# Two-block network on one core: gated attention's level differences one level ahead, one Ln and Exp for two tiles, feed-forward norm tile by tile

## What is computed

```python
def hybrid_layer(x, ...):
    h = rms_norm(x, norm_mix)
    proj = h @ w_in                      # queries, keys, values, gates of four mixers
    y_nsa, y_sb, y_gla, y_fox = ...      # four attention mixers
    branch = jnp.einsum('bsnc,ncd->bsnd', ys, w_branch)
    gates = jax.nn.sigmoid(gate_logits + b_gate)
    x = x + jnp.sum(gates * branch, axis=2) @ w_out
    h2 = rms_norm(x, norm_ff)
    return x + jnp.square(jax.nn.relu(h2 @ w_ff1)) @ w_ff2
```

## Time and profile before

| what | us |
|---|---|
| median of 3 runs | 2266.33 |
| the profiled execution's own time | 2267.46 |
| its span in the profile | 2265.7 |
| VectorE busy | 1250.2 (55%) |
| ScalarE busy | 675.4 (30%) |
| GpSimd busy | 480.4 (21%) |

### The profile page before, as it was taken

The page is one execution under the profiler, slowest core; times in us unless marked ns, Lnnn a source line. Parts: engine busy times, 40 slices in busy tenths (PEclk is TensorE's granted clock), DMA queues, the critical chain, the costliest instruction groups (busy, mean ns, idle before and its releaser), DMA issues.

```text
span 2265.7 us, 32730 instructions
## 1 busy us (share of the span) xinstructions
PE 2185.9 (96%) x13766; PEld 1777.7 (78%) x13766; DVE 1250.2 (55%) x1678; ACT 675.4 (30%) x1496; POOL 480.4 (21%) x259
## 2 busy tenths in 40 slices
PE   7999999999999999999999999999999999998998
PEld 7998878889889987788898745557888886556987
DVE  5576445855455765448654316664434434456666
ACT  2224453032012234450330267622112012362111
POOL 2222112323322221123233000101111110101332
PEclk9999999999999999999999999999999999999999
DMA  9533666645465336676546403022232223213551
GB/s 264 182 121 119 254 248 194 246 149 223 168 171 207 136 126 222 229 238 218 191 183 218 172 0 118 1 74 93 75 111 84 102 65 85 86 62 120 196 186 56
DMA packets 225958, 339.57 MB, mean 150 GB/s; under 512 B 58987, under 2 KB 94806, under 8 KB 225814
## 3 DMA queue, kind: packets, MB, share of 16 engines
q1 hardware_dynamic: 224720, 333.98, 42.7%
q0 software_dynamic: 944, 3.47, 0.4%
q10 hardware_dynamic: 150, 0.04, 0.0%
HBM read 335.38 MB, written 2.10 MB: 149 GB/s over the span
## 4 chain that ended last, share of the span: by engine, by line
PE 58%; DVE 3%; ACT 2%; issue 1%; POOL 0%; DVEq 0%; ACTq 0%; POOLq 0%
PE bank L2118 15%; PE bank L282 13%; PE bank L284 13%; PE bank L283 13%; PE bank L2121 2%; PE bank L655 2%; DVE ring_low L270 1%; PE bank L1000 1%; ACT work L1134 1%; PE bank L658 1%; PE bank L952 0%; ACT work L2419 0%; DVE work L1693 0%; ACT work L2517 0%; ACT L1134 0%
## 5 line engine op out<-in xcount | busy, mean ns | idle before, releaser
L283 PE MATMUL bank<-hT_high,ring_low 128*128 128x256 f32 (+1 forms) x2048 | 608.3, 297 | 0.0
L283 PEld LDWEIGHTS bank<-hT_high,ring_low 128*128 128x128 f32 x2048 | 393.4, 192 | 12.1 <-issue 0.7
L263 POOL CAST ring_high<-ring 128x2048 fp32r<-128x2048 f32 (+1 forms) x108 | 204.1, 1890 | 685.8 <-PE bank L284 620.7
L282 PE MATMUL bank<-hT_low,ring_high 128*128 128x256 f32 (+1 forms) x1008 | 296.6, 294 | 7.5 <-DVE ring_low L270 4.5
L270 DVE TENSOR_TENSOR ring_low<-ring,ring_high 128x2048 fp32r<-128x2048 f32 (+1 forms) x108 | 242.1, 2244 | 98.4 <-POOL ring_high L263 98.2
L284 PE MATMUL bank<-hT_high,ring_high 128*128 128x256 f32 (+1 forms) x1008 | 286.4, 284 | 0.0
L263 POOL CAST half_high<-ring 128x2048 fp32r<-128x2048 f32 x64 | 128.4, 2009 | 638.2 <-PE bank L284 465.4
L282 PE MATMUL bank<-ring_low,hidden_high 128*128 128x512 f32 x640 | 251.4, 393 | 0.0
L1134 ACT ACTIVATE work<-bank 128x384 f32<-128x384 f32 (+11 forms) x246 | 109.4, 466 | 364.5 <-PE bank L284 314.8
L282 PEld LDWEIGHTS bank<-hT_low,ring_high 128*128 128x128 f32 (+1 forms) x1008 | 193.5, 192 | 16.7 <-issue 9.2
L270 DVE TENSOR_TENSOR ring_low<-ring,half_high 128x2048 fp32r<-128x2048 f32 x64 | 152.7, 2390 | 97.0 <-POOL half_high L263 96.6
(11 more groups left out here) (242 smaller groups left out, 4424.3 us busy)
## 6 DMA issues: line engine op xcount, KB each, us to landing
ring<-w_ff SPq DMA_DIRECT2D x32, 2048.0 KB, 8.2
ring<-mlp_w SPq DMA_DIRECT2D x32, 2048.0 KB, 8.0
ring<-w_in SPq DMA_DIRECT2D x30, 2048.0 KB, 8.6
ring<-w_ada SPq DMA_DIRECT2D x20, 2048.0 KB, 8.9
ring<-w_branch SPq DMA_DIRECT2D x24, 512.0 KB, 6.4
ring<-w_in SPq DMA_DIRECT2D x32, 256.0 KB, 4.2
ring<-w_out SPq DMA_DIRECT2D x4, 2048.0 KB, 8.8
work<-w_ada SPq DMA_DIRECT2D x4, 2048.0 KB, 13.5
```

The costliest lines, as they stand in the source:

```text
L263: nc.gpsimd.tensor_copy(self.high(i), self.part(i, False)).then_inc(self.high_made, 1)
L282: nc.tensor.matmul(out, a[0], b[1], start=start, stop=False)
L283: nc.tensor.matmul(out, a[1], b[0], start=False, stop=False)
```

## The change

1. `prepare(n)` is cut into `decay(n)`, the difference, and `scale_qk(n)`, the scalings. The difference of the next level is issued right behind the scalings of a level, ahead of the low half and the merge.
2. ScalarE takes Ln and Exp of the gated output's statistics once for both tiles, after the squares of tile 1; VectorE's scaling of both tiles waits for that one event.
3. Norm of the feed-forward: `take_hT` and `low_bits` go tile by tile; ScalarE copies the modulation sums after them; TensorE's `turn_ada` (and the rows) come behind the first product of up0.
4. VectorE makes only low half 0 ahead of `add_out(1, 0)`, half 1 behind the low parts; GpSimd's casts of halves 2 and 3 wait for the scaled tile 1 instead of `wo11`.
5. Second block: the semaphore `kpe_zero` is replaced by a count on `kpe_ready`.

```diff
@@ tensor
         turn_x("yT", 1, TT + 2, xn)
-        turn_ada()
-        if l == DEPTH - 1:
-            pe.wait_ge(rows3_in, 2 * 16)
-            turn(OT.claim(pe, "rows3")[:, 0:N_ROWS3], rows3[0:N_ROWS3, :]).then_inc(OT.full, 1)
         arrived = columns("yT", 6)
...
                 last.then_inc(PROJ.full, 1)
+                if i + b == 0:
+                    turn_ada()
+                    if l == DEPTH - 1:
+                        pe.wait_ge(rows3_in, 2 * 16)
+                        turn(OT.claim(pe, "rows3")[:, 0:N_ROWS3], rows3[0:N_ROWS3, :]).then_inc(OT.full, 1)
@@ scalar
-            link(f(gl_stat[:, t], gl_stat[:, t], ACT.Ln, scale=1.0 / GLA_DV, bias=eps))
-            f(gl_rstd[:, t], gl_stat[:, t], ACT.Exp, scale=-0.5).then_inc(gl_scale, 1)
+        link(f(gl_stat, gl_stat, ACT.Ln, scale=1.0 / GLA_DV, bias=eps))
+        f(gl_rstd, gl_stat, ACT.Exp, scale=-0.5).then_inc(gl_scale, 1)
...
         row_scale(lambda t: PROJ.taken(act, f"wo0{t}", f"wo1{t}"), sq)
+        for t in range(TT):
+            for c in range(2):
+                take_hT("yT", ROW_FF, hT_high[1], c, t)
         ps = OT.arrived(act, "ada")
         copy(ada_sums, ps[:, :]).then_inc(OT.free("ada"), 1)
-        for c in range(2):
-            for t in range(TT):
-                take_hT("yT", ROW_FF, hT_high[1], c, t)
@@ gpsimd
-        pool.wait_ge(*done("wo11"))
+        pool.wait_ge(xn_ready, TT + 2)
@@ vector
-        prepared = [0]
-
-        def prepare(n):
-            h, k = LEVELS[n], prepared[0]
-            prepared[0] += 1
+        prepared = [n for n in range(len(LEVELS)) if LEVELS[n] > 0]
+
+        def decay(n):
+
+            h, k = LEVELS[n], prepared.index(n)
...
                               b[:, :, h - 1:h].to_broadcast([P, 512 // (2 * h), 2 * h]), ALU.subtract).then_inc(lv_diff, 1)
+
+        def scale_qk(n):
+
+            k = prepared.index(n)
+            d = lv_d[:, k % 2]
             dve.wait_ge(lv_exp, k + 1)
...
-        prepare(0)
+        decay(0)
         Y.make_low(nc, dve, 15)
-        prepare(2)
-        for n in range(2):
-            Y.make_low(nc, dve, 16 + n)
-            merge(n)
+        scale_qk(0)
+        decay(2)
+        Y.make_low(nc, dve, 16)
+        scale_qk(2)
+        merge(0)
+        decay(3)
+        Y.make_low(nc, dve, 17)
+        merge(1)
         for n in range(3, len(LEVELS)):
-            prepare(n)
+            scale_qk(n)
+            if n + 1 < len(LEVELS):
+                decay(n + 1)
             Y.make_low(nc, dve, 15 + n)
             merge(n - 1)
...
-            dve.wait_ge(gl_scale, t + 1)
+            dve.wait_ge(gl_scale, 1)
...
-        X.make_low(nc, dve, 0, 1)
+        X.make_low(nc, dve, 0)
         add_out(1, 0)
         norm(0, TT + 1, xn)
         add_out(1, 1)
         norm(1, TT + 2, xn)
-        for c in range(2):
-            low_bits("yT", ROW_FF, hT_high[1], c)
-        X.make_low(nc, dve, 2, 3)
+        for t in range(TT):
+            for c in range(2):
+                low_bits("yT", ROW_FF, hT_high[1], c, t, TT * KD + (TT * t + c) * 4)
+        X.make_low(nc, dve, 1, 2, 3)
```

More of the change, by code:

```diff
@@ L1420, in sigmoid, with low_bits @@
             link(vec.reciprocal(e, e))
[L1422 to L1435, removed]
+        def low_bits(name, row, high, c, t, rounded_before):
+            ps = TURN[t].arrived(dve, f"{name}{t}{c}")
+            dve.wait_ge(hT_rounded, rounded_before + 4)
+            for k in range(4):
+                at, part = row + 4 * c + k, slice(t * P, (t + 1) * P)
+                last = vec.scalar_tensor_tensor(hT_low[:, 4 * c + k, part], ps[:, k * P:(k + 1) * P], cols[:, at:at + 1],
+                                                high[:, 4 * c + k, part].bitcast(F32), ALU.mult, ALU.subtract)
+                if k == 3:
+                    last.then_inc(TURN[t].free(f"{name}{t}{c}"), 1)
+                elif t == TT - 1:
+                    last.then_inc(hT_cut, 1)
         if l > 0:
@@ L1442, in vector @@
         for c in range(2):
-            low_bits("xT", ROW_MIX, hT_high[0], c)
+            for t in range(TT):
+                low_bits("xT", ROW_MIX, hT_high[0], c, t, (TT * c + t) * 4)
             if l == 0 or c == 1:
@@ L2066, in second_block @@
     kpe_ready = sem("kpe_ready")
-    kpe_zero = sem("kpe_zero")
+    KPE_ZEROED, KPE_ROTATED = 1, 2
     ln_order = [(i, j, t) for i in range(DEPTH) for j in range(2) for t in range(NT[i])]
@@ L2246, in mla_project @@
                     PT.taken(pe, "1sumk")
-                    pe.wait_ge(kpe_zero, 1)
+                    pe.wait_ge(kpe_ready, KPE_ZEROED)
                     pe.wait_ge(grid_in, 16)
@@ L2670, in mla_project @@
         def mla_project():
-            vec.memset(m_kpe[0:HD, :], 0.0).then_inc(kpe_zero, 1)
+            vec.memset(m_kpe[0:HD, :], 0.0).then_inc(kpe_ready, 1)
             for t in range(TT):
@@ L2687, in mla_project @@
                    lambda ps: ps[pe_rows, 0:S]).then_inc(kpe_ready, 1)
-            dve.wait_ge(kpe_ready, 1)
+            dve.wait_ge(kpe_ready, KPE_ROTATED)
             for j in range(1, 8, 2):
@@ L2875, in gpsimd @@
         norm_rows(1, 0, whole_count[0, 1, TT - 1])
-        pool.wait_ge(kpe_ready, 1)
+        pool.wait_ge(kpe_ready, KPE_ROTATED)
         for n in range(4):
```

## The result

The changed kernel takes 2248.05 us (median of 4 runs, 2246.20 to 2249.92) against 2265.65 us (4 runs): ratio 0.993, interval 0.9913 to 0.9947. Six more runs of it in a later experiment gave 2247.43 us and 0.9919 (0.9903 to 0.9935). So it is faster by some 18 us; forecast were 20.6 us and 2247 us.

The account below looks back on a forecast made before the run. TensorE bounds the kernel, busy for 2185.9 us, so only its idle time can be won. 3.4 + 1.4 + 7.3 + 8.5 = 20.6 us off 2267.46 gives 2246.9, said as 2247 us; range 2241 to 2259.

Parts of the forecast that it names:

- Levels: Gated-attention levels: the earlier difference shortens TensorE's waits for VectorE's merges, 1.7 us a layer, 3.4 us in all.
- some 0.5 us of the 1.13 stay: TensorE's wait before level 8: the merge of level 7 still comes late, leaving some 0.5 us of 1.13.
- my walk: VectorE's new queue in the levels followed through the old cast times, each low half behind its cast, to date the merges.
- Statistics: Gated output: two table loads, one Ln, one Exp fewer; TensorE's 0.42 and 0.30 us waits go, 1.4 us in all.
- Norm: Feed-forward norm: TensorE's idle before the first product falls to 1.1 us in each layer, 7.3 us together.
- the first low part at 459.4, and TensorE starts at 459.5: Layer 0, first feed-forward product: it starts right after tile 1's first low part, with 1.1 us idle.
- Clock: TensorE's half-clock stretches behind the waits in levels and norm: 10.2 us as upper bound, 8.5 us taken as gain.
- Rival (a): The idle goes and the clock still falls: 2255.4 us at worst, 2251 where half stays; chance 0.2.
- (b): Feed-forward norm: GpSimd's casts, released with tile 1's scaled rows, hold the low parts of hT; 2260 us, chance 0.05.
- (d): Slower: differences and scalings meet a cast at each level, some 13 us more a layer, 2276 us; chance 0.03.

Follow-up runs that it names:

- levels_only: Kernel before with the difference of a level issued one level ahead, nothing else: 2258.39 us against 2264.47, ratio 0.9977 (0.9966 to 0.9988).
- own_banks: Changed kernel with tile 1 turned into the two SC banks instead of PROJ's: median 2246.08 us of five, ratio 0.9914 to the kernel before.
- stats_only: Kernel before with one Ln and one Exp for both tiles of the gated output, nothing else: 2261.70 us, ratio 0.9991 (0.9980 to 1.0001).

## Why the prediction was right, and where its terms were not

The direction, the size and the range were right: 2247 forecast, 2248.05 and 2247.43 measured. That the time was met so closely is in part luck: the sum hides errors that cancel in part, and its 20.6 us, 3 too many, were taken off one execution that lay 1.8 us above the median of four (2267.46 against 2265.65).

- **Levels: 3.4 us forecast; 4.6 us of waits for merges and 1.84 us of waits for ScalarE's bank gone.** The step "some 0.5 us of the 1.13 stay" failed: the changed kernel and levels_only have no wait at level 8. In levels_only the merge of level 7 starts 4.1 us behind the end of its cast; my walk had 5.2, since it put the whole piece of the compressed branch, 1.7 us, behind the cast, while 0.6 us of it ran ahead and only 0.7 us were left behind it. And the walk looked at VectorE's and TensorE's own waits only; the label "issue" hid ScalarE's bank.
- **Statistics: 1.4 us**, as forecast, by the profile. The reading behind it was off in one place: three of the four instructions had a table load ahead, not all four; two loads a layer are gone all the same.
- **Norm: 7.3 us of idle forecast, 5.4 gone** (4.73 and 4.78 us to 2.07 each). The step "the first low part at 459.4, and TensorE starts at 459.5" failed. The product claims the PROJ bank that holds tile 1's turned rows, and so waits for the fourth low part; own_banks gave 0.72 of the missing 0.97 us back. The steps before it held: the additions, the 0.75 us scaling, both turns without waits. From the end of the output products to the first feed-forward product it is 7.9 us, where 7.1 were forecast.
- **Clock: 8.5 us forecast, about 2.6 measured, give or take 1.2.** This is the term that was most off. Even if all the 10.2 us of lost clock in those stretches had gone, at 0.61 they would have brought 6.2. The profiled execution of before had falls behind level 8 in both layers and behind both norms. I took them as the waits' price in every run. In stats_only, which keeps the waits at levels 7 and 8 (1.01 and 1.19 us, level 8 at 182.56), the stretch in question is

```profile
182.00:188.00 6.00, 5.44 (x48) 5.35 (x49) 4.59 (x5) 0.01 (x1) 1.53 (x1) 1.00 0.01 3
```

  at full clock, and so is the one behind level 8:

```profile
184.00:190.00 6.00, 6.00 (x51) 5.88 (x50) 3.22 (x3) 0.00 (x0) 0.00 (x0) 1.00 0.00 0
```

  And of the changed kernel's two profiles one has no fall behind the norms (the stretch 452 to 462 has 1.00), the other has 0.57 over 455 to 459 in layer 0, behind the same wait of 2.07 us. So the same program has a fall behind the same wait in one execution and none in the other; what settles it no run here shows. Falls also came where the kernel before had none. At the passage to layer 1 it has 1.00 over 640 to 660, the changed kernel

```profile
639.00:647.00 8.00, 6.23 (x32) 5.87 (x33) 6.94 (x19) 3.55 (x14) 0.00 (x0) 0.57 1.14 252
```

  Over 636 to 654 eight of the nine profiles with the new norm have a fall (all but own_banks), the three with the old norm have none. Rival (a), that the clock still falls, was half true: some falls went, some came elsewhere.
- **What is not accounted for.** Waits gone: 6.4 + 1.4 + 5.4 = 13.2 us; clock 2.6; together 15.8 of some 18 us. The lines at equal clock give 15.7 us instead of 13.2; this difference of some 2 us is more than they are off by with one slope, and stays open. It may be the price of the clock: 0.64 is a mean over the whole kernel, and at a full microsecond for each lost one the clock would bring 4.1 us and leave 1 open. No run shows which.
- **Rivals.** (b), the casts holding the low parts of hT: no; the casts now run from 452.25 on beside them and sixteen parts take 4.3 us, before 4.2. (d), slower by holds in the levels: the holds are there, in layer 0 four of 2.38 us and two shorter ones, but at most one a level and for the most part under the cast that the queue waits for in any case.

## What to carry to other kernels

When an engine in strict order waits a fixed time for its own helper, move the request one step ahead; here eight exponentials a layer were asked for earlier with nothing added, and TensorE got back more than its waits for VectorE (4.6 us), since ScalarE's queue stood behind VectorE's too (1.84 us). A bank or buffer that is claimed earlier than it is needed can turn into a wait that names nobody, as the six labelled issue did here: claim it ahead of its first use, and count every claim on the path when a start is computed. And take a clock fall seen in one execution as a chance, not as a price: compare it over several runs before it enters a sum.

## What was not expected of the hardware

- A cast of GpSimd holds not only VectorE instructions with two SBUF tensors. In the changed kernel a `tensor_scalar` on eight values beside a cast took 1.61 us, others of it 0.17:

```profile
163.82 0.17 DVE L1578 TENSOR_SCALAR work<-work 128x8 f32<-128x8 f32 x1
...
172.45 1.61 DVE L1578 TENSOR_SCALAR work<-work 128x8 f32<-128x8 f32 x1
```

  while low parts of hT, which read PSUM and SBUF, kept their 0.27 us beside two casts. The Trainium skill (GPSIMD Engine Reference, Specifications) names two-port modes beside two SBUF inputs. The trace fits that, though it doesn't show the mode; the price is the rest of the cast, 1.59 us.
- With the same program the mean granted clock of whole runs of the kernel before lay between 0.986 and 0.994, and their times between 2259.4 and 2269.0 us: most of the scatter of this kernel's times goes with the clock.
